# Two of the four weight-block sums of each gate/up slab move from VectorE to the DMA queues

## The reference, cut to what matters

```
def swiglu(x, w_gu, w_down):
    g, u = jnp.split(x @ w_gu, 2, axis=-1)       # w_gu: 1024 x 5632
    return (jax.nn.silu(g) * u) @ w_down         # w_down: 2816 x 1024
...
x = layer_norm(ALPHA * x + 0.5 * swiglu(x, ffn1_w_gu[l], ffn1_w_down[l]), ...)
x = layer_norm(ALPHA * x + hybrid_mixer(x, ...), ...)
x = layer_norm(ALPHA * x + 0.5 * swiglu(x, ffn2_w_gu[l], ffn2_w_down[l]), ...)
```

## Time and profile before

| | |
|---|---|
| median of 3 runs | 2360.7 us (2360.57 to 2362.52) |
| the profiled execution's own time | 2362.68 us |
| its span, first to last instruction | 2360.9 us |
| PE busy | 2329.8 us (99%) |
| DVE busy | 1566.9 us (66%) |
| ACT busy | 970.1 us (41%) |
| POOL busy | 19.1 us (1%) |
| moved by DMA | 247.08 MB, mean 105 GB/s |
| mean granted TensorE clock | 0.994 of full speed |

### The profile page before, as it was taken

How to read it: one execution, slowest core, us unless ns; L and a number is a source line. 1 busy time by engine, 2 the same in 40 slices (tenths; PEclk the granted TensorE clock), 3 DMA queues, 4 the chain that set the end, 5 groups by cost and what they waited for, 6 DMA issues and landing times.

```text
span 2360.9 us, 34887 instructions
## 1 busy us (share of the span) xinstructions
PE 2329.8 (99%) x14416; PEld 2098.5 (89%) x14416; DVE 1566.9 (66%) x2262; ACT 970.1 (41%) x1497; POOL 19.1 (1%) x16
## 2 busy tenths in 40 slices
PE   8999999999999999999999999999999999999998
PEld 8999888888888899998899998898888888999987
DVE  7888546554654688883588883565455637888834
ACT  5445324434442344443244443243344433444521
POOL 0000300000000000000000000000000000000000
PEclk9999999999999999999999999999999999999999
DMA  5333434323233333333233333243223233233332
GB/s 152 108 108 108 147 105 134 94 72 99 89 94 119 113 90 106 101 116 107 89 90 103 101 120 107 87 139 101 79 94 98 90 107 125 76 104 108 121 111 73
DMA packets 295053, 247.08 MB, mean 105 GB/s; under 512 B 13136, under 2 KB 256880, under 8 KB 294896
## 3 DMA queue, kind: packets, MB, share of 16 engines
q1 hardware_dynamic: 294352, 244.34, 33.5%
q10 hardware_dynamic: 544, 0.52, 0.1%
HBM read 238.51 MB, written 6.31 MB: 104 GB/s over the span
## 4 chain that ended last, share of the span: by engine, by line
PE 97%; DVE 2%; issue 1%; ACT 0%; DMA 0%; DVEq 0%
PE main L1581 10%; PE main L1583 10%; PE main L1582 10%; PE side L1735 6%; PE side L1736 6%; PE side L1737 6%; PE main L1736 6%; PE main L1735 6%; PE main L1737 6%; PE main L1687 5%; PE main L1689 5%; PE main L1688 5%; PE side L1688 4%; PE side L1689 4%; PE side L1687 4%; PE main L1670 1%
## 5 line engine op out<-in xcount | busy, mean ns | idle before, releaser
L990 DVE TENSOR_TENSOR wl<-raw,wh 128x1024 fp32r<-128x1024 f32 (+2 forms) x277 | 305.8, 1146 | 447.9 <-ACT wh L649 447.6
L649 ACT ACTIVATE wh<-raw 128x1024 fp32r<-128x1024 f32 (+2 forms) x277 | 260.8, 994 | 319.2 <-PE side L1689 175.2
L1581 PE MATMUL main<-xh,wh 128*128 128x512 f32 x848 | 334.4, 394 | 0.0
L1583 PE MATMUL main<-xl,wh 128*128 128x512 f32 x848 | 330.4, 390 | 0.0
L1582 PE MATMUL main<-xh,wl 128*128 128x512 f32 x848 | 330.2, 389 | 0.0
L733 ACT ACTIVATE wh<-tw 128x1024 fp32r<-128x1024 f32 x80 | 84.8, 1059 | 254.2 <-PE side L1737 130.4
L1583 PEld LDWEIGHTS main<-xl,wh 128*128 128x128 f32 x848 | 159.1, 188 | 33.7
L1581 PEld LDWEIGHTS main<-xh,wh 128*128 128x128 f32 x848 | 159.2, 188 | 33.3 <-issue 0.3
L1582 PEld LDWEIGHTS main<-xh,wl 128*128 128x128 f32 x848 | 159.3, 188 | 31.8
L1735 PE MATMUL side<-sum_hi,wh 128*128 128x256 f32 x640 | 183.3, 286 | 0.0
L1736 PE MATMUL side<-sum_hi,wl 128*128 128x256 f32 x640 | 183.2, 286 | 0.0
(11 more groups left out here) (302 smaller groups left out, 5726.0 us busy)
## 6 DMA issues: line engine op xcount, KB each, us to landing
raw<-gu SPq DMA_DIRECT2D x326, 256.0 KB, 4.0
raw<-w_in SPq DMA_DIRECT2D x100, 512.0 KB, 4.6
raw<-down SPq DMA_DIRECT2D x80, 512.0 KB, 4.6
raw<-w_branch SPq DMA_DIRECT2D x24, 512.0 KB, 4.6
raw<-w_out SPq DMA_DIRECT2D x16, 512.0 KB, 4.3
raw<-w_in SPq DMA_DIRECT2D x28, 256.0 KB, 3.3
raw<-gu SPq DMA_DIRECT2D x13, 512.0 KB, 6.2
raw<-down SPq DMA_DIRECT2D x16, 256.0 KB, 2.8
```

Of the source, the lines that this page charges most:

```text
L649: ins = act.activation(put(wh[block_of(g)]), get(raw[slot]), ACT.Copy)
L990: ins = V.tensor_tensor(put(wl[b]), get(raw[slot]), f32(put(wh[b])), ALU.subtract)
L1581: T.matmul(out, hi, rh(k), start=k == 0, stop=False)
L1583: ins = T.matmul(out, hi, rl(k), start=False, stop=k == kk - 1)
```

## The change

Sums 1 and 3 are no longer made by DVE. SP loads W01 twice, into `raw[slot][1536:2048]` and into `tw[:, slot]`, and the other three blocks as before. GpSimd then issues transfers that add onto what lies there (`accum_op=ALU.add`): W00 onto the first, W11 onto the second, each as two transfers of 128 KB on one semaphore (`t1_in`, `t3_in`). GpSimd waits for the first raw half before the first pair, and for `t3_begun` before the second. Both sums are now sums and not differences, and the signs of the token sums and of the combining steps are turned to match. ACT and DVE handle sums 1 and 3 in two instructions of 512 columns each, instead of one of 1024. SP waits for `slab_done` of the stage before, ahead of the first load into `tw` of each stage but the first. `angles()` runs on GpSimd after the sums of the first stage.

```
 def gate_and_up(g, gu, layer, c):
+    n0 = g - c
     slot = g % 2
     sp.wait_ge(w_lo.sem, 2 * g - 2)
+    sp.dma_start(raw[slot][:, 1536:2048]..., part_of_gate_up(gu, layer, c, 0, 1)).then_inc(raw_in[slot][0].sem, 16)
+    if n0 and c == 2:
+        sp.wait_ge(slab_done.sem, n0)
+    sp.dma_start(tw[:, slot, :]..., part_of_gate_up(gu, layer, c, 0, 1)).then_inc(t3_begun[slot].sem, 16)
-    for i, (half_, j) in enumerate(((0, 1), (0, 0), (1, 1), (1, 0))):
+    for i, (half_, j) in enumerate(((0, 0), (1, 1), (1, 0))):
         sp.dma_start(raw[slot][:, 512 * i:512 * i + 512]..., ...).then_inc(raw_in[slot][half_].sem, 16)
...
 # ACT, sums_13
-    act.wait_ge(t13_ready.sem, sum_no(g) + 1)
-    act.activation(wh[...][:, 0:1024], tw[:, 0:2, :]..., ACT.Copy).then_inc(*o.up(t13_hi))
+    act.wait_ge(t1_in[g % 2].sem, dma_sums(g))
+    act.activation(wh[...][:, 0:512], raw[g % 2][:, 1536:2048], ACT.Copy).then_inc(*o.up(t13_hi))
+    act.wait_ge(t3_in[g % 2].sem, dma_sums(g))
+    act.activation(wh[...][:, 512:1024], tw[:, g % 2, :], ACT.Copy).then_inc(*o.up(t13_hi))
...
+def block_sums(layer, f, n):                                   # GpSimd
+    pool.wait_ge(raw_in[slot][0].sem, arrived[g])
+    for h in range(2):
+        G.dma_start(raw[slot][:, 1536 + 256 * h:1792 + 256 * h]..., b11[:, 2 * h:2 * h + 2, :], accum_op=ALU.add).then_inc(t1_in[slot].sem, 16)
+    pool.wait_ge(t3_begun[slot].sem, dma_sums(g) // 2)
+    for h in range(2):
+        G.dma_start(tw[:, slot, 256 * h:256 * h + 256]..., b22[:, 2 * h:2 * h + 2, :], accum_op=ALU.add).then_inc(t3_in[slot].sem, 16)
...
 # DVE
-def sums_13(g): ...                        # one TENSOR_TENSOR, 1024 columns, for each slab
 def sum_2(g):
+    dve.wait_ge(t1_in[g % 2].sem, dma_sums(g))
     ...
 def low_13(g):                             # two TENSOR_TENSOR of 512 columns instead of one of 1024
...
 # PE, seven
-    pe.wait_ge(t13_lo.sem, i + 1)
+    pe.wait_ge(t13_lo.sem, 2 * i + 1)
     multiply(bank(1)[:, second], b, 0, (sums_hi[0], sums_lo[0])).then_inc(product.sem, 1)
     pe.wait_ge(sum_lo_ready.sem, 4 * v + 2)
+    pe.wait_ge(t13_lo.sem, 2 * i + 2)
     multiply(bank(2)[:, first], b, 1, (sums_hi[1], sums_lo[1])).then_inc(product.sem, 1)
```

More of the change, by code:

```diff
@@ L297, in build @@
         sum_lo_ready = Signal("sum_lo_ready")
-        t13_ready = Signal("t13_ready")
+        t1_in = [Signal(f"t1_in{i}") for i in range(2)]
+        t3_begun = [Signal(f"t3_begun{i}") for i in range(2)]
+        t3_in = [Signal(f"t3_in{i}") for i in range(2)]
         t2_ready = Signal("t2_ready")
@@ L443, in sum_product, with dma_sums, part_of_gate_up @@
             return 5 * sum_no(g) + j + 1
+        def dma_sums(g):
+            return 32 * (sum_no(g) // 2 + 1)
+        def part_of_gate_up(gu, layer, c, half_, j):
+            w = gu[layer].rearrange("(k p) n -> p k n", p=P)
+            return w[:, 4 * half_:4 * half_ + 4, c * P + j * DFF:c * P + j * DFF + P]
         arrived, so_far = [], [0, 0]
@@ L520, in gate_and_up @@
             def gate_and_up(g, gu, layer, c):
+                n0 = g - c
                 slot = g % 2
                 sp.wait_ge(w_lo.sem, 2 * g - 2)
-                w = tiles(gu, layer)
-                for i, (half_, j) in enumerate(((0, 1), (0, 0), (1, 1), (1, 0))):
+                sp.dma_start(raw[slot][:, 1536:2048].rearrange("p (k c) -> p k c", c=P),
+                             part_of_gate_up(gu, layer, c, 0, 1)).then_inc(raw_in[slot][0].sem, 16)
+                if n0 and c == 2:
+                    sp.wait_ge(slab_done.sem, n0)
+                sp.dma_start(tw[:, slot, :].rearrange("p (k c) -> p k c", c=P),
+                             part_of_gate_up(gu, layer, c, 0, 1)).then_inc(t3_begun[slot].sem, 16)
+                for i, (half_, j) in enumerate(((0, 0), (1, 1), (1, 0))):
                     sp.dma_start(raw[slot][:, 512 * i:512 * i + 512].rearrange("p (k c) -> p k c", c=P),
-                                 w[:, 4 * half_:4 * half_ + 4, c * P + j * DFF:c * P + j * DFF + P]).then_inc(raw_in[slot][half_].sem, 16)
+                                 part_of_gate_up(gu, layer, c, half_, j)).then_inc(raw_in[slot][half_].sem, 16)
             def rows(layer, j):
@@ L715, in plain_blocks @@
                     act.wait_ge(raw_in[g % 2][h].sem, arrived[g])
-                act.activation(wh[sum_blocks(g)[1]][:, 0:1536], raw[g % 2][:, 512:2048], ACT.Copy).then_inc(*o.up(w_hi))
+                act.activation(wh[sum_blocks(g)[1]][:, 0:1536], raw[g % 2][:, 0:1536], ACT.Copy).then_inc(*o.up(w_hi))
             def sums_13(g, first):
@@ L723, in sums_13 @@
                     act.wait_ge(product.sem, sum_product(g - 1, 2))
-                act.wait_ge(t13_ready.sem, sum_no(g) + 1)
-                act.activation(wh[sum_blocks(g)[0]][:, 0:1024], tw[:, 0:2, :].rearrange("p a c -> p (a c)"),
-                               ACT.Copy).then_inc(*o.up(t13_hi))
+                act.wait_ge(t1_in[g % 2].sem, dma_sums(g))
+                act.activation(wh[sum_blocks(g)[0]][:, 0:512], raw[g % 2][:, 1536:2048], ACT.Copy).then_inc(*o.up(t13_hi))
+                act.wait_ge(t3_in[g % 2].sem, dma_sums(g))
+                act.activation(wh[sum_blocks(g)[0]][:, 512:1024], tw[:, g % 2, :], ACT.Copy).then_inc(*o.up(t13_hi))
             def sums_24(g, first):
@@ L975, in angles @@
                 then(G.tensor_scalar(an, an, 3.1415925, -3.1415925, ALU.min, ALU.max), angles_ready)
-            angles()
+            def block_sums(layer, f, n):
+                g = layer * S_LAYER + f * (S_FFN + S_MIX) + n
+                slot, gu = g % 2, (gu1, gu2)[f]
+                b11, b22 = (part_of_gate_up(gu, layer, n, i, i) for i in range(2))
+                pool.wait_ge(raw_in[slot][0].sem, arrived[g])
+                for h in range(2):
+                    G.dma_start(raw[slot][:, 1536 + 256 * h:1792 + 256 * h].rearrange("p (k c) -> p k c", c=P),
+                                b11[:, 2 * h:2 * h + 2, :], accum_op=ALU.add).then_inc(t1_in[slot].sem, 16)
+                pool.wait_ge(t3_begun[slot].sem, dma_sums(g) // 2)
+                for h in range(2):
+                    G.dma_start(tw[:, slot, 256 * h:256 * h + 256].rearrange("p (k c) -> p k c", c=P),
+                                b22[:, 2 * h:2 * h + 2, :], accum_op=ALU.add).then_inc(t3_in[slot].sem, 16)
+            for layer in range(DEPTH):
+                for f in range(2):
+                    for n in range(2, KF):
+                        block_sums(layer, f, n)
+                    if layer + f == 0:
+                        angles()
         @block.vector
@@ L1092, in norm_tail, with sum_2 @@
                     low(L + 1, 3)
-            def sums_13(g):
-                for h in range(2):
-                    dve.wait_ge(raw_in[g % 2][h].sem, arrived[g])
+            def sum_2(g):
+                dve.wait_ge(t1_in[g % 2].sem, dma_sums(g))
+                dve.wait_ge(raw_in[g % 2][1].sem, arrived[g])
                 if sum_no(g):
-                    dve.wait_ge(t13_lo.sem, sum_no(g))
                     dve.wait_ge(w_lo.sem, 2 * g)
[L1101 to L1107, removed]
+                V.tensor_tensor(tw[:, 2, :], raw[g % 2][:, 512:1024], raw[g % 2][:, 1536:2048], ALU.add).then_inc(*o.up(t2_ready))
             def sum_4(g):
                 dve.wait_ge(t2_ready.sem, sum_no(g) + 1)
-                V.tensor_tensor(tw[:, 3, :], raw[g % 2][:, 1536:2048], tw[:, 2, :], ALU.subtract).then_inc(*o.up(t4_ready))
+                V.tensor_tensor(tw[:, 3, :], raw[g % 2][:, 1024:1536], tw[:, 2, :], ALU.add).then_inc(*o.up(t4_ready))
             def plain_low(g):
@@ L1115, in plain_low @@
                 dve.wait_ge(w_hi.sem, 2 * g + 1)
-                V.tensor_tensor(wl[b][:, 0:1536], raw[g % 2][:, 512:2048], f32(wh[b][:, 0:1536]), ALU.subtract).then_inc(*o.up(w_lo))
+                V.tensor_tensor(wl[b][:, 0:1536], raw[g % 2][:, 0:1536], f32(wh[b][:, 0:1536]), ALU.subtract).then_inc(*o.up(w_lo))
             def low_13(g):
                 b = sum_blocks(g)[0]
-                dve.wait_ge(t13_hi.sem, sum_no(g) + 1)
-                V.tensor_tensor(wl[b][:, 0:1024], tw[:, 0:2, :].rearrange("p a c -> p (a c)"), f32(wh[b][:, 0:1024]),
+                dve.wait_ge(t13_hi.sem, 2 * sum_no(g) + 1)
+                V.tensor_tensor(wl[b][:, 0:512], raw[g % 2][:, 1536:2048], f32(wh[b][:, 0:512]),
+                                ALU.subtract).then_inc(*o.up(t13_lo))
+                dve.wait_ge(t13_hi.sem, 2 * sum_no(g) + 2)
+                V.tensor_tensor(wl[b][:, 512:1024], tw[:, g % 2, :], f32(wh[b][:, 512:1024]),
                                 ALU.subtract).then_inc(*o.up(t13_lo))
@@ L1137, in token_sums @@
                         dve.wait_ge(x1_in[h].sem, 16)
-                V.tensor_tensor(sums_x[0][:, :, :], a21, a22, ALU.add).then_inc(*o.up(sum_ready))
+                V.tensor_tensor(sums_x[0][:, :, :], a21, a22, ALU.subtract).then_inc(*o.up(sum_ready))
```

(8 more changed lines are left out.)

## The result

The changed kernel takes 2909.1 us (median of 4 runs, 2907.1 to 2912.9) against 2360.7 for the kernel before (median of 3 runs; a fourth, at 2547 us, was disturbed and is left out). The ratio is 1.232, interval 1.230 to 1.234: 548 us slower. Forecast were 2648, at most 2850. The profiled execution took 2912.9 us, with a span of 2911.1 and a mean granted clock of 0.919.

The account below looks back on a forecast made before the run. PE was taken to bound the kernel, busy 2329.8 of 2360.9 us. Losses of 212 us in three stages and 76.5 in the first, less 1, gave +287 and 2648 us, range 2358 to 2850.

Parts of the forecast that it names:

- one by one: GpSimd's four adds a slab never overlap, so a slab takes 14.24 us, more than PE's 10.08.
- where it shows: Expected profile: slabs about 14 us apart, PE idle ahead of product 2 or 3, DVE busy about 1480 us.
- SP's wait for `slab_done`: Before a stage's first load into `tw`: already met when PE ends the slab before, costing nothing.
- The gain at the stage starts: At three later stage starts, 0.4 us gained less 0.06 each: -1 us in all, at most 3.4.
- What they take: Price of each 128 KB add on GpSimd's queue: 2.6 + 0.46 + 0.5 = 3.56 us.
- The sum: Gate/up stages: 17 later groups lose 4.16 us each, 212 us over three stages, 76.5 in the first; total +287.
- The range: Whole kernel: 2358 to 2850 us, leaving out transfers above 4.2 us and (d).
- the likeliest case: GpSimd's adds run one by one at 3.0 to 4.6 us each; chance 0.69.
- (a): Rival: GpSimd's adds overlap and cost nothing, 2360 us; chance 0.14.
- (c): Rival: the DMA engines are the limit, 11.9 us a slab at four times an add's plain 0.46, 2480 us; chance 0.08.
- (b): Rival: GpSimd's adds run one by one at 2.6 us, 10.4 us a slab, 2364 us; chance 0.07.
- (d): Rival: faster by over 4.7 us, though L1102's share at the stage starts is at most 3.4 us; chance 0.02.

Follow-up runs that it names:

- runs 1 and 2: The changed kernel with reserved descriptor room raised from 1024 bytes to 1088 (2613.9 us) and to 1792 (2452.9 us).
- run 3: The changed kernel at 1024 bytes, with a separate semaphore for each half of a sum: 2904.6 us.
- plain kernel: The changed kernel at 1024 bytes, with GpSimd's half-block transfers overwriting instead of adding: 2361.1 us.
- run 5: The changed kernel at 1024 bytes, with SP's five loads cut to a quarter from group 4 of each stage on: 2797.0 us.
- runs 2 and 6: The changed kernel with 1792 bytes, with whole SP loads (2452.9 us) and with loads cut to a quarter from group 4 of each stage (2361.8 us).

## Why the prediction was right or wrong

**Right: one by one, and GpSimd's queue sets the pace.** The adds do not overlap, and runs 1 and 2 show that the reserved room is the reason; run 3 excludes the semaphore. The most that were in flight at once in the whole traces: of adds of 256 rows one with 1024 bytes, two with 1088, three with 1792; of adds of 128 rows three with 1024; of plain transfers with 1024 bytes three of 256 rows, but only one of 512. If each transfer takes a fixed part of the room, these counts give an estimate of the part: over 512 bytes for an add of 256 rows (two do not fit in 1024) and at most 544 (two fit in 1088); over 256 and at most 341 both for an add of 128 rows and for a plain transfer of 256; over 512 for a plain one of 512. So an add behaves like a plain transfer of twice its rows, and it is the part of the room that decides, and not the adding as such. What that part consists of, no run shows.

**Right: where it shows.** PE idles ahead of products 2 and 3, DVE waits for ACT and ACT for a DMA, DVE is at 1489 us (forecast about 1480). The clock falls, from 0.994 to 0.919 of full speed in the mean, and it should cost nothing of its own (argued, not isolated): from 100 to 150 us the chain has only "issue" and the two lines of GpSimd's adds, and no work of PE. SP's wait for `slab_done` shows in no row of its waits, and L537 still waits for DVE, 1074.7 us in 72 pieces. `angles` waited 28.8 us for its input instead of 254.1 and held nothing up. The gain at the stage starts is as small as forecast. The chain of the plain kernel, where the transfers cost nothing, has `tw` behind ACT's high part, as expected:

```profile
844.62 1.50 ACT wh L734
...
847.82 0.69 DVE tw L1137
...
854.58 0.36 PE side L1766
```

From the start of ACT's copy to PE's first matmul are 854.58 - 844.62 = 9.96 us; before they were 855.55 - 845.29 = 10.26. That is 0.30 us won, where I had 0.4 less 0.06. Three times this is about what I summed as 1 us, and too little to be seen in the times: plain is at 0.9997 of the kernel before, with 1 within the interval.

**Wrong: "What they take", the price of an add.** The mechanism was right, and this term of the sum was too small: 3.56 us where 4.37 were measured. I had 2.6 + 0.46 + 0.5 = 3.56 us. The landing, 3.7 in the median, was close; two things were missing. Until the next issue pass another 0.3 us: in run 5 the add of 101.46 landed after 3.53 us and the next was issued at 105.32, so that undisturbed adds are 3.85 apart. And the sum took the adds as alone on the DMA engines, though five blocks from SP must land in every slab. The page gives the mean distances: 421.8 / 156 + 1.22 = 3.92 us ahead of L1003 and 576.3 / 160 + 1.22 = 4.82 ahead of L1007, together 2 x 8.74 = 17.5 us a slab and 4.37 an add, with single ones at 5.9. That is 3.2 us a slab more than my 14.24. Of it 4 x 0.29 = 1.2 are the undisturbed price, 1.5 went away with three quarters of SP's loads (run 5), and 0.6 is what is left in run 5 above four undisturbed adds (16.0 - 4 x 3.85), the loads' last quarter among it.

**The sum, redone.** A slab loses 17.5 - 10.08 = 7.4 us instead of 4.16. 548 / 7.4 are 74 slabs, 18.5 a stage. The forecast had 17 in the later stages, because at 3.56 us an add group 4 came just in time; at 4.37 it is 9.6 us late. The first `seven` slab began at 41.87 instead of 35.59 (36.10 in the plain kernel): `hp` of group 0 (L1205, at 41.08) stands on DVE behind the low part of sum 3, which waited 5.12 us behind the fourth serial add. Had I put 4.37 for 3.56, the same sum would have given 2907. That is a check of its form and no forecast, since 4.37 is read from the result.

**The range** ended at 4.2 us an add, although the likeliest case was itself written as 3.0 to 4.6 us, which holds the 4.37. The row for more was there: landings of up to 8.0 us for SP's own blocks, an effect of sharing that I used for the first stage alone.

**The rivals.** (a) needed overlapping adds and fell with the timeline. Room for three did not bring 2360 either: it brought 2453, because the landings in the traffic of SP's loads make the loop of a raw buffer longer than two slabs (runs 2 and 6). (c), full DMA engines, does not show in the windows from 60 to 200 us: their share is 0.53 with 1024 bytes, which is 0.53 x 17.5 = 9.3 us of work a slab and under 10.08, and 0.79 with 1792. It was not far off, though: an add takes 1.07 us of all 16 engines (below), and the rival begins above 1.37. (b), one by one at 2.6 us, fell with the price: no add of the change landed in under 3.3 us. Plain transfers reach 2361.1 us, but they overlap, so they do not speak for (b). A plain transfer of GpSimd landed after 2.8 us in the median, an add after 3.7. (d) is closed as far as tried: no version was faster. Room for four whole adds in flight was not tried.

## What to carry to other kernels

Before work moves to transfers that GpSimd issues, find out how many of them the reserved room lets run at once (here one add of 256 rows with 1024 bytes, two with 1088, three with 1792): that decides how many overlap, and no wait in the profile names it (it reads "issue"). Do not count on a new transfer as soon as the oldest has landed: here it also waited for the second, or for all. Then price each transfer in the traffic that it will run in, not alone, and compare it with two limits: the rate (transfers a slab by their distance) and the deadline of the first one that is needed. Moving work from an engine that is not the bound can win very little; here DVE's 78 us bought 0.3 us at a stage start where the transfers cost nothing.

## What was not expected of the hardware

- An add of 128 KB in 256 rows of 512 bytes holds GpSimd for 1.22 us, a plain transfer of the same rows for 0.72; one of 64 KB 0.86, and a plain one of 512 rows only 0.75. Adding makes the issue grow with the rows: 128 more cost 0.36 us in an add, and 256 more 0.03 in a plain one.
- An add costs the DMA engines more than twice what a plain transfer of the same bytes does. In the change GpSimd's queue q0 took 11.8% of 2911.1 us for 320 adds, 1.07 us of all 16 engines each. In the plain kernel the row is

```profile
q0 software_dynamic: 15360, 41.96, 6.3%
```

  and 6.3% of 2358.6 us for 320 transfers are 0.46 each. The packets differ as well: 87040 are 17 for each add on each of 16 engines, where its 256 rows are 16 on each; 15360 are only 3 for each plain transfer. So a price for each packet (0.118 x 16 x 2911.1 / 87040 = 63 ns in an add) can't be carried from one kind to the other.
- GpSimd does not go on as soon as the oldest transfer has landed: with 1088 bytes reserved, where two adds fit, it waited for both in flight (104.33 after a landing at 104.1), and the eight adds of 64 KB went in fours.
- An add that meets a burst of SP's loads can land some 2 us later (5.9 us to the next issue instead of 3.85), and with room for one everything behind it moves by as much.
